# Folding the pooling maps into w_out's blocks, and moving layer 0's rotations and first states earlier, in a two-layer streaming encoder

## What is computed

```python
hn = rmsnorm(x, g_mix)
proj = hn @ w_in
u_a, u_b = proj[..., :512], proj[..., 512:]
y_a = s5_mixer(u_a)        # 32 groups, 64 complex states each, gelu, half-GLU
# pool_mixer, 4 groups k of 128 channels, trailing windows 2, 4, 8, 16:
diff = pooled - u_b
y_b = einsum('blkc,kcd->blkd', diff, w_pool) * scale
x = x + concat([y_a, y_b]) @ w_out
x = x + square(relu(rmsnorm(x, g_ffn) @ w_ff1)) @ w_ff2
```

## Time and profile before

| | |
|---|---|
| Runs | 2159.89, 2159.79, 2155.44 us; median 2159.79 |
| Profiled execution, its own time | 2159.76 us |
| Its span | 2157.9 us |
| PE busy | 2085.5 us (97%) |
| DVE busy | 1092.7 us (51%) |
| ACT busy | 439.2 us (20%) |
| POOL busy | 145.0 us (7%) |
| Mean granted PE clock over the span | 0.993 |

### The profile page before, as it was taken

The page is one execution under the profiler, slowest core; times in us unless marked ns, Lnnn a source line. Parts: engine busy times, 40 slices in busy tenths (PEclk is TensorE's granted clock), DMA queues, the critical chain, the costliest instruction groups (busy, mean ns, idle before and its releaser), DMA issues.

```text
span 2157.9 us, 29004 instructions
## 1 busy us (share of the span) xinstructions
PE 2085.5 (97%) x12894; PEld 2044.8 (95%) x12894; DVE 1092.7 (51%) x1459; ACT 439.2 (20%) x525; POOL 145.0 (7%) x171
## 2 busy tenths in 40 slices
PE   6989899999999999999999999999999999999997
PEld 6878899999999999999989899999999999999997
DVE  7889555364644435353466745643333434343346
ACT  5222342020111111011232233311010101111112
POOL 0022020000000000000020300200000000000003
PEclk9999999999999999999999999999999999999998
DMA  4526311111111121113124461111111111111112
GB/s 151 153 85 171 93 49 45 49 44 46 69 62 59 49 62 59 51 59 121 68 103 129 120 186 39 40 49 40 49 40 49 43 46 44 45 46 43 48 41 83
DMA packets 68861, 152.64 MB, mean 71 GB/s; under 512 B 8288, under 2 KB 28544, under 8 KB 68352
## 3 DMA queue, kind: packets, MB, share of 16 engines
q1 hardware_dynamic: 49264, 112.63, 16.6%
q0 software_dynamic: 7664, 24.65, 3.8%
q10 hardware_dynamic: 11808, 13.51, 2.1%
HBM read 123.23 MB, written 27.53 MB: 70 GB/s over the span
## 4 chain that ended last, share of the span: by engine, by line
PE 82%; DVE 10%; ACT 4%; issue 2%; DMA 1%; ACTq 0%; SPq 0%; DVEq 0%
PE tile L448 77%; PE tile L714 2%; DVE h_low L1037 2%; DVE x L1384 2%; DVE w_low L1033 1%; ACT h_high L763 1%; ACT w_high L748 1%; DVE dve_products_late L1023 1%; DVE pool_s L1023 1%; PE small L616 1%; PE small L610 1%; DMA w_raw<-w_blocks 1%; PE small L501 1%; DVE states L1023 0%; DVE prep_products L1023 0%
## 5 line engine op out<-in xcount | busy, mean ns | idle before, releaser
L448 PE MATMUL tile<-h_high,w_high 128*128 128x408 f32 (+1 forms) x1920 | 427.5, 331 | 22.3 <-DVE h_low L1037 19.6
L1384 DVE TENSOR_TENSOR x<-tile,x 128x816 f32<-128x816 f32 (+1 forms) x304 | 205.7, 718 | 456.1 <-PE tile L448 440.2
L448 PE MATMUL tile<-h_low,w_high 128*128 128x408 f32 (+1 forms) x1920 | 423.1, 328 | 0.0
L448 PE MATMUL tile<-h_high,w_low 128*128 128x408 f32 (+1 forms) x1920 | 422.8, 328 | 0.0
L448 PEld LDWEIGHTS tile<-h_high,w_high 128*128 128x128 f32 x1920 | 320.9, 188 | 28.6 <-issue 19.0
L748 ACT ACTIVATE w_high<-w_raw 128x1024 fp32r<-128x1024 f32 x162 | 170.4, 1052 | 746.6 <-PE tile L448 728.6
L448 PEld LDWEIGHTS tile<-h_low,w_high 128*128 128x128 f32 x1920 | 320.6, 188 | 1.1
L448 PEld LDWEIGHTS tile<-h_high,w_low 128*128 128x128 f32 x1920 | 320.4, 188 | 1.0
L448 PE MATMUL tile<-hidden_high,w_high 128*128 128x408 f32 (+1 forms) x1440 | 318.3, 329 | 2.1 <-DVE x L1384 1.2
L448 PE MATMUL tile<-hidden_low,w_high 128*128 128x408 f32 (+1 forms) x1440 | 316.3, 328 | 0.0
L448 PE MATMUL tile<-hidden_high,w_low 128*128 128x408 f32 (+1 forms) x1440 | 316.3, 328 | 0.0
(11 more groups left out here) (195 smaller groups left out, 1670.5 us busy)
## 6 DMA issues: line engine op xcount, KB each, us to landing
w_raw<-w_blocks SPq DMA_DIRECT2D x164, 512.0 KB, 3.5
x<-x_t ACTq DMA_DIRECT2D x8, 544.0 KB, 11.6
u_blocks<-ua_dram SPq DMA_DIRECT2D x64, 68.0 KB, 2.7
ya_dram<-u_blocks ACTq DMA_DIRECT2D x64, 68.0 KB, 2.7
y_a<-ya_dram POOLq DMA_DIRECT2D x8, 544.0 KB, 4.4
x_kept<-x ACTq DMA_DIRECT2D x8, 544.0 KB, 2.7
cy_dram<-y_quarter POOLq DMA_DIRECT2D x16, 256.0 KB, 2.9
carry_weights<-cy_dram POOLq DMA_DIRECT2D x8, 512.0 KB, 6.8
```

The costliest lines, as they stand in the source:

```text
L448: mm = pe.matmul(ps[tile][:, c, 0:(b - a) * J], lhs, xt[:, k, a * J:b * J], start=(first and n == 0), stop=(last and n == 2))
L1384: ins = v.tensor_tensor(xt, pt_, xt, ALU.add)
```

## The change

The pooled map of a group is followed by a scale and by w_out's rows for that group, with nothing else between, so the product of the three can be made in advance. The new kernel transposes the four `w_pool` maps on PE (`mixes`, after tile 5), scales them while ACT copies them back, and multiplies them into each of the four w_out blocks as they lie in `w_raw` (`fold(i)`: four fp32 products of 256 columns per block); ACT copies the result over the raw block (`fold_out`) before `split_hi`. The pool products and the y_b steps go. In their place ACT rounds the differences themselves (`pooled_high`, `dhi`) and DVE makes their low part (`pooled_low`, `dlo`). PE runs the first two `wob` tiles interleaved, k = 3, 2, 1 of both and then k = 0 of both. `fold(0)` stands after tile 6, `fold(1)` after tile 7, `fold(2)` and `fold(3)` among the `wob`s, and the orders on PE, ACT and DVE around them change. In layer 0 `rotations(0, 1)`, `rotations(0, 2)` and `pre(0, 0)` stand earlier in DVE's order. SP waits for the last squares of x before it loads the maps and the identity; POOL's last two loads of x also wait for `fold(3)`.

```diff
--- before.py
+++ after.py
 NC = 2 * FFC
 NB = B_FF + 2 * KD * FFC
 
...
+        def folded(slot, half):
+
+            return slot.rearrange("p (n k m) -> p k n m", n=2, k=KA)[:, 2 * half:2 * half + 2]
+
+        def no_gaps(k):
+
+            for f, g in ((slice(0, JP), slice(2, JP + 2)), (slice(JP, J), slice(JP + 4, J + 4))):
+                yield (lambda flat: flat[:, k, :].rearrange("p (t j) -> p t j", j=J)[:, :, f]), ub[:, k, :, g]
+
...
+                        sp.wait_ge(sq_made, 16 * l + 8)
                         if l:
                             sp.wait_ge(x_kept, 16 * KD)
                         sp.dma_start(wp[:, :, :].rearrange("p k d -> p (k d)"), w_pool[l]).then_inc(wp_in, 16)
+                        sp.dma_start(ident[:, :], prep_in[l, :, C_ID:C_ID + P]).then_inc(wp_in, 16)
                     if 4 <= b < 8:
                         turn_u(l, b - 4)
                     if b == B_WOB + 3:
-                        sp.wait_ge(tile_free, LT + T_POOL + KA + 2)
+                        sp.wait_ge(dlo_made, KA * (l + 1))
                         for m in range(6):
                             sp.dma_start(x[:, m, :], (x_in, x_hist)[l][m]).then_inc(x_back[m], 16)
...
+                def mixes():
+
+                    pe.wait_ge(wp_in, 32 * (l + 1))
+                    out = small_at(SM["mix", l])
+                    for k in range(KA):
+                        mm = pe.transpose(out[:, k * P:(k + 1) * P], wp[:, k, :], ident[:, :])
+                    mm.then_inc(small_done, 1)
+
+                def fold(i):
+
+                    b = LB + B_WOB + i
+                    pe.wait_ge(raw_landed[b % 2], 16 * (b // 2 + 1))
+                    if i == 0:
+                        pe.wait_ge(mix_made, l + 1)
+                    for half in range(2):
+                        out = small_at(SM["fold", l, i, half])
+                        for k in range(2):
+                            mm = pe.matmul(out[:, k * 2 * P:(k + 1) * 2 * P], wp[:, 2 * half + k, :],
+                                           folded(raw[:, b % 2, :], half)[:, k], start=True, stop=True)
+                        mm.then_inc(small_done, 1)
...
+                        if t == 5:
+                            mixes()
                     elif 2 <= t < 6:
                         drives(1, t - 2)
-
-                pe.wait_ge(wp_in, 16 * (l + 1))
-                for i in range(KA):
-                    k = KA - 1 - i
-                    tile_at(LT + T_POOL + i)
-                    pe.wait_ge(diff_made, l * KA + i + 1)
-                    for c, (a, b) in enumerate(CHUNKS):
-                        out = ps[i % 2][:, c, 0:(b - a) * J].rearrange("p (t j) -> p t j", j=J)
-                        pe.matmul(out[:, :, 0:JP], wp[:, k, :], ub[:, k, a:b, 2:2 + JP], start=True, stop=True)
-                        mm = pe.matmul(out[:, :, JP:J], wp[:, k, :], ub[:, k, a:b, JP + 4:J + 4],
-                                       start=True, stop=True)
-                    mm.then_inc(tile_done, 1)
+                        if t == 5:
+                            mixes()
+                    if t >= KD - 2:
+                        fold(t - (KD - 2))
...
                 def wob(n):
-                    half_tile(B_WOB, T_WOB, n, ybh, ybl, None if n else
-                              lambda k: pe.wait_ge(tile_free, LT + T_POOL + KA - k + 2), True)
+                    half_tile(B_WOB, T_WOB, n, dhi, dlo)
+
+                def first_wobs():
+
+                    block_at(LB + B_WOB)
+                    for n in range(2):
+                        tile_at(LT + T_WOB + n)
+                        for k in range(KA - 1, 0, -1):
+                            if n == 0:
+                                pe.wait_ge(dlo_made, l * KA + KA - k)
+                            products(n, 0, KA * n + k, k, dhi, dlo, k == KA - 1, False)
+
+                def first_wobs_end():
+                    pe.wait_ge(dlo_made, l * KA + KA)
+                    for n in range(2):
+                        products(n, 0, KA * n, 0, dhi, dlo, False, True).then_inc(tile_done, 1)
 
                 def carry(q):
 
-                    if q == 0:
-                        pe.wait_ge(small_free, SM["drive", l, GP - 1] + 1 + 2)
-                        if l == 0:
-                            pe.wait_ge(small_free, SM["kernel", 0, 3, 1] + 1 + 2)
+
+                    pe.wait_ge(small_free, SM["fold", l, ((2, 3, 3, 3), (1, 2, 3, 3))[l][q], 1] + 1 + 2)
...
                 if l == 0:
-                    wob(0)
-                    wob(1)
+                    first_wobs()
+                    first_wobs_end()
+                    fold(2)
                     wob(2)
+                    wob(3)
                     carry(0)
-                    wob(3)
                     wob(4)
+                    pe.wait_ge(carry_free, 4)
+                    fold(3)
+                    wob(5)
                     carry(1)
-                    wob(5)
+                    wob(6)
                     carry(2)
-                    wob(6)
                     carry(3)
                     wob(7)
                 else:
                     carry(0)
-                    wob(0)
+                    first_wobs()
+                    first_wobs_end()
+                    pe.wait_ge(carry_free, GP + 4)
+                    fold(2)
+                    wob(2)
                     carry(1)
-                    wob(1)
-                    wob(2)
+                    wob(3)
+                    pe.wait_ge(carry_free, GP + 8)
+                    fold(3)
+                    wob(4)
                     carry(2)
-                    wob(3)
-                    wob(4)
+                    wob(5)
                     carry(3)
-                    for n in range(5, 8):
-                        wob(n)
+                    wob(6)
+                    wob(7)
...
+            def fold_out(l, i):
+
+                b = l * NB + B_WOB + i
+                for half in range(2):
+                    n = SM["fold", l, i, half]
+                    act.wait_ge(small_done, n + 1)
+                    act.activation(folded(raw[:, b % 2, :], half),
+                                   sm[n % 2][:, :].rearrange("p (k n m) -> p k n m", k=2, n=2),
+                                   ACT.Copy).then_inc(small_free, 1)
+                act.wait_ge(small_free, n + 1 + 2)
...
+            def mixes(l):
+
+                act.wait_ge(lp_in, 16 * (l + 1))
+                n = SM["mix", l]
+                act.wait_ge(small_done, n + 1)
+                for k in range(KA):
+                    act.activation(wp[:, k, :], sm[n % 2][:, k * P:(k + 1) * P], ACT.Copy,
+                                   scale=lp[:, L_SCALE + k:L_SCALE + k + 1]).then_inc(mix_step, 1)
+                act.wait_ge(mix_step, KA * (l + 1))
+                act.sem_inc(small_free, 1)
+                act.sem_inc(mix_made, 1)
...
+                def pooled_high(i):
+
+                    act.wait_ge(tile_done, LT + KD)
+                    act.wait_ge(diff_made, l * KA + i + 1)
+                    for at_cols, frames in no_gaps(KA - 1 - i):
+                        ins = act.activation(at_cols(dhi), frames, ACT.Copy)
...
-                    ahead(LB + t + 2, LT + t)
+                    if t < KD - 2:
+                        ahead(LB + t + 2, LT + t)
...
+                    if t == KD - 1:
+                        pooled_high(0)
...
+                        if t == 5:
+                            mixes(0)
...
+                        if t == 5:
+                            mixes(1)
+                    if l == 0 and t == KD - 1:
+                        pooled_high(1)
+                        pooled_high(2)
+                    if t >= KD - 2:
+                        fold_out(l, t - (KD - 2))
+                        ahead(LB + t + 2, LT + t)
+                for i in range((3, 1)[l], KA):
+                    pooled_high(i)
...
                 def wob_ahead(i):
+                    if i < 2:
+                        fold_out(l, i + 2)
                     ahead(LB + B_WOB + i + 2, LT + T_WOB + 2 * i + 1)
...
                     wob_ahead(1)
+                    wob_ahead(2)
                     carried(1)
-                    wob_ahead(2)
...
                     carried(0)
+                    wob_ahead(0)
                     carried(1)
-                    wob_ahead(0)
-                    carried(2)
                     wob_ahead(1)
                     gelus(0)
-                    carried(3)
+                    carried(2)
                     gelus(1)
                     wob_ahead(2)
+                    carried(3)
...
-                    if l:
+                    if l and t < KD - 2:
                         split_lo(LB + t + 2)
 
-                def y_b(i):
+                def pooled_low(i):
                     k = KA - 1 - i
-                    v.wait_ge(ybh_made, l * KA + i + 1)
```

(65 more changed lines are left out.)

33 lines of the change are left out of this document (22 added, 11 removed).

## The result

The changed kernel takes 2165.18 us (median of 6 runs, 2164.51 to 2167.42), the old one on the same chip 2158.74 (2155.44 to 2159.89). The ratio is 1.0033, 95% interval 1.0022 to 1.0043: by the ratio it is slower by 7.1 us, with 2.3 either way; the medians differ by 6.4. The forecast of 2166.0 us, slower, stands. Its parts are another matter, and they are read one by one.

The account below looks back on a forecast made before the run. It took PE to bound layer 1 and DVE, with PE just behind, to set layer 0's pace. The old 2159.76 us plus 0.8 for layer 0 and 5.4 for layer 1 gave 2166.0 us, range 2162 to 2169.

Parts of the forecast that it names:

- Start of carry(0), -1.0 us: Layer 1: carry(0) starts at 11.5 instead of 12.5 us after the old tile 7 end, waiting for POOL's transfers.
- Two folds, +4.2 us: Layer 1: fold(2) and fold(3) lie on PE's path and add 4.2 us.
- The clock, +2.2 us: Layer 1: after PE's 6.9 us wait, carry(0) starts at the low clock, costing 2.2 us, between 1.7 and 2.6.
- ACT's copies ... are done before PE asks for them: Layer 1: ACT's copies of the folded blocks are ready before PE needs them, so no added wait.
- Layer 0, DVE's chain: Layer 0: DVE reaches wob(0) 7.9 us earlier, then waits for x; last states at 227.4 instead of 228.45.
- Layer 0, +0.8 us: Layer 0 sum: carry(3) starts 1.4 us earlier but pays 2.2 us for the clock; bounds -5.7 and +3.5.
- the quick transfers: Rival, both layers: carry(0)'s last load and x[0] each land in 3.7 us; 2158.7 us, no change; chance 0.27.
- The one in which nothing waits at carry(0): Rival, layer 1: PE doesn't wait for carry(0)'s weights, layer 1 -3.7 us, total 2150.4 us, faster; chance 0.06.

Follow-up runs that it names:

- the filler: Changed kernel with 30 idle fp32 products on PE between fold(1) and carry(0) in layer 1: 2164.46 us, ratio 1.0022.
- the filler before carry(3): Changed kernel with layer 1's first half tiles before carry(0), layer 0's third-carry weights after x[1], plus 16 idle products before layer 0's carry(3): 2152.65 us, ratio 0.9968.
- POOL's hold: Changed kernel with POOL issuing the third carry's weights in layer 0 only once x[1] has landed: 2158.13 us, ratio 0.9997.
- other work put into the wait: Changed kernel with PE running layer 1's first two half tiles before carry(0): 2157.07 us, ratio 0.9995.
- the order of the loads: Changed kernel with layer 1's first half tiles before carry(0), and in layer 0 third-carry weights after x[1] and x loads before block 11: 2149.62 us, ratio 0.9957.

## Why the prediction was right

The total was right, the verdict too, and the mechanism in both layers: a wait for a transfer where the gain should have been. That the total came within 1 us is in part luck, since terms too large and terms left out made up for each other. The terms, against the traces:

- **Start of carry(0), -1.0 us.** Measured -1.7. Tile 7 ends 2.28 us later after the mark (72.90 against 70.62; forecast 2.5): 1.54 for `fold(0)`, which leaves 0.74 for `mixes`, forecast as 2.1 and 0.4. Carry(0) starts 8.50 us after the end of tile 7 (forecast 9.0) instead of 12.48. The choice of 4.0 for the last load's landing held (3.9), and so did its reason, the weight block no longer beside it.
- **Two folds, +4.2 us.** Over-sized: 3.1. I priced a 256-column product at 0.52 us, by the old pool products; four of the fold's take 1.54 us, 0.385 each. The two differ in how they read their operand (the pool product in short pieces with gaps, the fold in runs of 128), but whether that is the cause wasn't tried.
- **The clock, +2.2 us.** Carry(0) took 7.70 us, 2.5 more than 5.18 (7.06 to 7.21 in the three other profiles with this layer 1, whose second half was back at the full clock). As an amount it holds, as a term of its own it doesn't: with the filler the first half lost it, and ACT's copy took its place. The step that failed is "ACT's copies ... are done before PE asks for them": true of the folded blocks, but I hadn't asked it of carry(0)'s own copy, which stands behind `pooled_high(3)` and `decays`. So two waits end nearly together in layer 1, POOL's weights for the first half and ACT's copy for the second, and taking away the first alone uncovers the second. The condition that I set for the clock, a wait of over 3 us, was also off: with the filler a wait of 2.48 us was followed by the low clock, and in the old kernel's layer 1 one of 1.97 us was in one profile and not in the other.
- **Not forecast, +0.9 us.** Carry(2) of layer 1 waits 1.40 us for ACT where the old kernel shows 0.48:

```profile
1278.04 1.19 PE L664 MATMUL small<-u_blocks,intra_weights 128*128 128x136 f32 x8 [1.40 <-ACT u_blocks L1008]
```

- Sum of these for layer 1: -1.7 + 3.1 + 2.5 + 0.9 = 4.8 of the 5.22 in this pair of profiles.
- **Layer 0, DVE's chain.** I forecast `wob(0)` at 167.0 (measured: free at 166.7), x[0] issued at 164.2 (163.8), last states at 227.4 (227.8). The landing of x[0] was mis-sized: 8 us, with 9.3 as its bound, and 10.7 came; in three other profiles with the same layer 0 it was 9.4 to 9.8. That x[1] came with x[0] and not 3 us behind it made good for that: both adds were done at 177.1, forecast 176.5. Carry(3) then started 0.40 us behind the last states (227.79 to 228.19), which the sum took as nothing.
- **Layer 0, +0.8 us.** -0.7 for carry(3)'s start and +2.75 for its clock would be +2.1. At the first product by z the profile shows +2.20; 1.0 of that is gone by layer 1's mark, which shows +1.23. But three of the experiments leave layer 0 as the changed kernel has it, and their marks lie at 1143.43, 1144.86 and 1144.63 instead of 1146.91. The mean of the four is 1144.96, 0.7 before the old kernel's one mark. (Two of them were 1.7 us ahead of the others before x was asked for; without that the mean is 1145.8.) So layer 0's share is about nothing, to a microsecond or two, and not settled finer; nor is it settled how the measured 7.1 us (4.7 to 9.3) divide between the two layers. And as the filler before carry(3) showed, the clock's 1.5 us there seem mostly not on the path either, as far as one pair of profiles shows it.

Of the rivals, the quick transfers (2158.7) are what POOL's hold produces in layer 0: 2158.1 with layer 1 left as it was, more than this rival promised. The one in which nothing waits at carry(0) came close by another way: other work put into the wait, -5.7 us in layer 1.

The two rules of the Trainium skill: that of "TensorE: Matmul & The Clock Gate", section "Why this matters for your kernels", to leave no gaps between bursts, agrees with the rows (after waits of 6.61 and 3.72 us a carry's first group took 2.15 us, against 1.09 to 1.20 elsewhere). The rule speaks of longer gaps than the 2.48 us after which a group took 2.18, and the measurement decides. Filling a gap with idle products brought nothing measurable here, though. That of "DMA: Bandwidth & Descriptors", section "Bandwidth", gives 6.15 us for 1 MB, the DMA engines' time alone; carry(0)'s megabyte was in place 7.7 us after the first issue (1220.57 to 1228.3), of which 4.8 are issuing, so issuing was indeed the larger part.

## What to carry to other kernels

When work that hid a transfer is removed, the transfer sets the time: ask first what started the load and whether its start moves too. If it doesn't, put other ready work in the gap; here one call in another place was worth 5.7 us in its profile and 8.1 by the medians, and the order of the loads 7.5 us more by the medians (2157.07 to 2149.62). Time won on an engine ahead of a load that the same step triggers is worth only what the load's landing leaves of it, and the landing depends on the other queues at that moment. Look for a second wait right behind the one that you remove. Price a slow clock behind a wait only after asking what else is due there: what the clock costs may already be owed to another wait.

## What was not expected of the hardware

Six loads of 544 KB, asked for at 163.7 or 163.8 us by the same code, had their first one there after 10.7 us with POOL's eight loads of 64 KB and one of 512 KB being issued at the time (9.4 to 10.7 in five profiles), and after 4.7 us without these. Even the issuing on SP was slower beside them (up to 1640 ns for one, against 493). The same showed in small: 68 KB writes took 5.2 us beside two loads of x and one of `y_a`, and 2.5 us when they were sent 2.3 us later; what made the difference there wasn't tried by itself.
